# A sixth weight buffer in a three-layer float32 kernel, in SBUF given up by GpSimd's DMA scratch

## What is computed

```python
# twice (l = 0, 1)
mod = silu(c) @ w_ada[l] + b_ada[l]             # [2048] @ [2048, 6144]: shift, scale, gate
u = rms_norm(x, norm_w) * (1 + scale) + shift
proj = u @ w_in[l]                              # [256, 2048] @ [2048, 19064]
...                                             # two attentions, a state space scan, gates
merged = g0 * (y_fox @ w_o_fox) + g1 * (y_dsa @ w_o_dsa) + g2 * (y_ssd @ w_o_ssd)
x = x + gate * (merged @ w_out)
# once
z = rms_norm(x) @ w_in_2                        # [256, 2048] @ [2048, 13312]
...                                             # a two-sided recurrence, a windowed attention
x = x + rms_norm((m0 * (y_a @ w_proj_a) + m1 * (y_b @ w_proj_b)) @ w_out_2)
```

## Time and profile before

| | us |
|---|---|
| median of 3 runs | 3477.04 (3476.33 to 3477.14) |
| the profiled execution's own time | 3473.09 |
| its span on the profile | 3471.3 |
| PE busy | 3335.0 (96%) |
| DVE busy | 2238.9 (64%) |
| ACT busy | 1701.7 (49%) |
| POOL busy | 46.8 (1%) |
| load queue of SP | 675.38 MB, 52.5% of 16 DMA engines |

### The profile page before, as it was taken

The page is one execution under the profiler, slowest core; times in us unless marked ns, Lnnn a source line. Parts: engine busy times, 40 slices in busy tenths (PEclk is TensorE's granted clock), DMA queues, the critical chain, the costliest instruction groups (busy, mean ns, idle before and its releaser), DMA issues.

```text
span 3471.3 us, 43913 instructions
## 1 busy us (share of the span) xinstructions
PE 3335.0 (96%) x18250; PEld 2894.8 (83%) x18250; DVE 2238.9 (64%) x2687; ACT 1701.7 (49%) x2098; POOL 46.8 (1%) x90
## 2 busy tenths in 40 slices
PE   5799989989999999999999999999999999999998
PEld 4679978878888887799788878888888899988887
DVE  5688777866666556687666576655567776544544
ACT  3354565554434344546655544343446875434343
POOL 0000000000000000000000000000000000000000
PEclk8799999999999999999999999999999999999999
DMA  8654456556677655444544467765555443455554
GB/s 354 261 222 173 170 209 248 219 199 249 260 279 287 224 183 193 162 179 158 180 172 159 174 234 267 272 249 196 189 183 191 177 173 140 158 218 194 194 184 156
DMA packets 102918, 719.32 MB, mean 207 GB/s; under 512 B 12176, under 2 KB 12256, under 8 KB 18752
## 3 DMA queue, kind: packets, MB, share of 16 engines
q1 hardware_dynamic: 93888, 675.38, 52.5%
q0 software_dynamic: 8256, 37.64, 3.1%
q10 hardware_dynamic: 576, 3.50, 0.3%
HBM read 710.08 MB, written 6.40 MB: 206 GB/s over the span
## 4 chain that ended last, share of the span: by engine, by line
PE 86%; DVE 7%; ACT 3%; DMA 2%; issue 1%; SPq 0%; DVEq 0%; ACTq 0%
PE G L1214 79%; DVE LL L1812 3%; DMA RAW<-w_ada_turned_packed_dram 1%; PE BA L1362 1%; PE BD L1335 1%; DVE S L2019 1%; PE BD L1397 1%; DMA RAW<-in_w_in_packed_dram 1%; ACT HH L1455 1%; PE BC L1348 0%; DVE RAW L1823 0%; PE BE L1280 0%; PE BA L1416 0%; PE BC L1416 0%; PE BC L1380 0%
## 5 line engine op out<-in xcount | busy, mean ns | idle before, releaser
L1455 ACT ACTIVATE HH<-RAW 128x2048 fp32r<-128x2048 f32 x546 | 1044.7, 1914 | 1138.1 <-PE G L1214 838.4
L1812 DVE TENSOR_TENSOR LL<-RAW,HH 128x2048 fp32r<-128x2048 f32 x546 | 1247.8, 2287 | 357.8 <-ACT HH L1455 357.3
L1214 PE MATMUL G<-HH,UH 128*128 128x512 f32 x2560 | 1022.1, 399 | 61.2 <-DVE LL L1812 57.2
L1214 PE MATMUL G<-LL,UH 128*128 128x512 f32 x2560 | 1003.6, 392 | 0.0
L1214 PE MATMUL G<-HH,UL 128*128 128x512 f32 x2560 | 1003.3, 392 | 0.0
L1214 PEld LDWEIGHTS G<-HH,UH 128*128 128x128 f32 x2560 | 485.1, 189 | 171.0 <-DVE LL L1812 67.4
L1214 PE MATMUL G<-UH,HH 128*128 128x256 f32 x2080 | 602.9, 290 | 9.8 <-DVE XS L2055 7.2
L1214 PE MATMUL G<-UH,LL 128*128 128x256 f32 x2080 | 589.2, 283 | 0.0
L1214 PE MATMUL G<-UL,HH 128*128 128x256 f32 x2080 | 588.9, 283 | 0.0
L1214 PEld LDWEIGHTS G<-LL,UH 128*128 128x128 f32 x2560 | 484.5, 189 | 103.7
L1214 PEld LDWEIGHTS G<-HH,UL 128*128 128x128 f32 x2560 | 485.6, 190 | 100.6 <-issue 2.9
(11 more groups left out here) (336 smaller groups left out, 2304.2 us busy)
## 6 DMA issues: line engine op xcount, KB each, us to landing
RAW<-in_w_in_packed_dram SPq DMA_DIRECT2D x402, 1024.0 KB, 4.8
RAW<-w_ada_turned_packed_dram SPq DMA_DIRECT2D x88, 1024.0 KB, 4.9
RAW<-in_w_out_packed_dram SPq DMA_DIRECT2D x48, 1024.0 KB, 4.8
RAW<-in_w_o_ssd_packed_dram SPq DMA_DIRECT2D x32, 1024.0 KB, 4.8
RAW<-in_w_o_fox_packed_dram SPq DMA_DIRECT2D x16, 1024.0 KB, 4.8
RAW<-in_w_o_dsa_packed_dram SPq DMA_DIRECT2D x16, 1024.0 KB, 4.9
RAW<-in_w_proj_a_packed_dram SPq DMA_DIRECT2D x16, 1024.0 KB, 4.8
RAW<-in_w_proj_b_packed_dram SPq DMA_DIRECT2D x16, 1024.0 KB, 4.8
```

What stands on the lines that cost most here:

```text
L1214: mm = pe.matmul(to, lt, rh, start=first, stop=end, skip_group_check=True)
L1455: a.activation(HH[g % NH][:, :n], RAW[buf(ch["f"])][:, :n], ACT.Copy).then_inc(*hi_done.up(g))
L1812: v.tensor_tensor(LL[buf(f)][:, :n], RAW[buf(f)][:, :n], HH[g % NH][:, :n].bitcast(F32), ALU.subtract).then_inc(*lo_done.up(g))
```

## The change

```diff
@@ -28,7 +28,7 @@
 
 C_ID, C_PI, C_UM, C_CM, C_IF, C_ONE, C_FR, C_END = 0, 128, 256, 384, 640, 641, 642, 690
 
-NR, NX, NH = 5, 3, 3
+NR, NX, NH = 6, 3, 3
 
 
 ON_PE = 2
@@ -2466,7 +2466,7 @@
     import concourse.bacc as bacc
     from concourse.bass_utils import run_bass_kernel_spmd
 
-    nc = bacc.Bacc("TRN2", target_bir_lowering=False, num_devices=1)
+    nc = bacc.Bacc("TRN2", target_bir_lowering=False, num_devices=1, dynamic_dma_scratch_size=8192)
     arrays, args = {}, {}
     given = laid_out(inputs)
     for name, arr in given.items():
```

## The result

The changed kernel takes **3448.44 us** (median of 4 runs, 3447.71 to 3450.18), the kernel before beside it 3476.68 (4 runs, 3471.77 to 3477.14). The ratio is 0.9924, 95% interval 0.9912 to 0.9935. The profiled execution took 3450.18 us.

The account below looks back on a forecast made before the run. PE, busy 3335.0 of 3471.3 us, was taken as the bound, with only gaps ending in late loads winnable. 7.5 + 13.2 - 1.0 = 19.7 us off the median of 3477.0 gave 3457.3 us; range 3451 to 3470.

Parts of the forecast that it names:

- What bounds the kernel: Whole kernel: PE bounds it; a buffer wins only PE idle time ending with a late load, in the opening and layer 0.
- The opening: Groups two to four of the opening: each ends 2.52 us earlier as its last loads land sooner, 7.5 us in all.
- Layer 0: Six places in layer 0 where a chunk's late load reaches PE: 13.2 us in all.
- 2.0 of the 2.97 go: Chunk 54 in layer 0: 2.0 us of PE's gap of 2.97 us would go.
- I take 3.0: Chunk 89 in layer 0: PE's gap of 2.88 us goes whole, with a trace of the next, 3.0 us.
- Chunks 84, 93 and 107: Layer 0: gains of 0.6, 3.5 and 2.8 us on PE; the prediction called the middle one chunk 94.
- Chunk 15: Layer 0: of PE's gap of 2.55 us, 1.3 us would be won.
- Take off 1 for what I have missed: Layer 0's sum: 1 us subtracted from the gain for anything missed.
- 1: Rival: only the opening wins, as `HH` holds ACT back and DVE fills layer 0's gaps; 3469.5 us, chance 0.12.
- 2: Rival: only layer 0 wins, as PE's second dot or full DMA engines limit the opening; 3463.8 us, chance 0.10.
- 3: Rival: nothing to see, under 7 us in all, both gains at half strength; about 3473 us, chance 0.09.
- 4: Rival: slower, as POOL waits for room in the halved scratch during the state space scan; 3495 us, chance 0.05.

Follow-up runs that it names:

- x5: Changed kernel, but six layer 0 loads (for chunks 15, 54, 84, 89, 94 and 107) wait as with five buffers; 3466.29 us, 0.9974 of the kernel before.
- x7: Kernel before with its five weight buffers, and the 8 KB spent on a fourth `HH`; 3473.03 us, 0.9994 of the kernel before.
- x1: The changed kernel again, nothing altered, timed beside the kernel before; 3448.72 us, ratio 0.9926.
- x3: Changed kernel with the sixth buffer used in the opening alone, five buffers afterwards; 3465.76 us, 0.9975 of the kernel before.
- x6: Changed kernel, but load 96 alone (chunk 54) waits as it would with five buffers; 3458.86 us, 0.9953 of the kernel before.
- x9: x6 plus 24 matmuls for nobody, run by PE in the gap ahead of the late head's transposes; 3455.58 us, 0.9939 of the kernel before.
- x10: Changed kernel, but load 168 alone, the ada load ahead of chunk 107's, waits as with five buffers; 3452.98 us, 0.9933 of the kernel before.
- x2: Kernel before with five buffers, only the scratch cut to 8192 bytes; 3474.15 us, 0.9999 of the kernel before.
- x4: Changed kernel with the sixth buffer used only after the opening; 3456.55 us, 0.9948 of the kernel before.
- x11: x8 with five buffers in place of six; 3458.09 us, 0.9949 of the kernel before.
- x8: Changed kernel, but in the opening PE's first dot of the next group stands ahead of the group's gemm; 3437.96 us, 0.9894 of the kernel before.

## Why the prediction was too careful

**What bounds the kernel: right.** The split into places where a load reaches PE and places where `HH` holds ACT anyway is borne out by x5 (few loads carry all of layer 0) and x7 (the larger wait was worth nothing). Layers 1 and 2 didn't move, and the stretch from 860 to 1130 is as busy as it was.

**The opening: right.** 7.5 forecast, 7.1 measured, 7.7 in x1 and 7.8 in x3. The fourth gemm starts at 126.48 in place of 134.19 (7.71 earlier) and ends only 6.81 earlier: it now runs more of its time at the low clock (0.60 on average in the 8 us from its start, against 0.74 before, in the windows above).

**Layer 0: the step that failed.** The text had "PE wins what lies behind it up to its next limit" and took the length of a gap as its price. That mis-sized two terms, "2.0 of the 2.97 go" at chunk 54 and "I take 3.0" at chunk 89. Measured are 5.1 and 4.8. By idle time alone both would be 2.5, close to the text; the rest is the halved clock behind each gap, 0.57 to 0.84 in the windows of before and 1.00 after. x6 brought gap and clock back at chunk 54 (5.4 us), x9 the gap without the clock (3.2). Chunks 84, 93 and 107 came as forecast (0.9, 3.3, 3.1 against 0.6, 3.5, 2.8). At 84 and 107 there was no low clock. At 93 idle time went from 6.4 us to 3.3, and a stretch at half clock of 3.4 us remains in place of 6.8; next to nothing came of that, as 3.1 of the 3.3 are idle time. Two of these hits are partly luck, as the two places also vary among kernels whose loads wait as before: 107 by 1.3 to 1.7 us (x10), 93 by 1.4 (x2, x3). Chunk 15 was put at 1.3 and gave -0.5 or 1.1, by where the stretch at low clock fell. Chunks 51 and 63 gave back 0.3 and 0.5, since a stretch at low clock came to them. The clock stood among the rows, and no term of the sum priced it.

**"Take off 1 for what I have missed": wrong in sign.** What was missed lay on the other side. Layer 0 was 12.2 with it and 15.8 by the trace, the whole 19.7 against 22.9.

**The scale: 4 us.** The text added the distance of one profiled execution of before to a median of three runs (3473.1 to 3477.0) to the result. After the change the profiled execution lies 1.7 us above its median, so 5.7 of the 8.9 us between 3457.3 and 3448.44 are this offset, and 3.2 are the sum's. In 19, 21 and 9 further runs the kernel before had medians of 3474.98, 3475.53 and 3475.76, from 3471.4 to 3480. The offset was scatter, not a property to carry over, and the low end of the range should have allowed for it.

**The rivals.** 1 and 2 fell by x3 and x4, 3 by the result, 4 by x2. The Trainium skill's rule on the descriptor carveout ("Debugging Trainium Hangs", section 4) didn't come into play: with 8192 bytes for 64 transfers the kernel ran in the same time (x2). No run shows how full the area was.

## What to carry to other kernels

Look for what a wait holds up, not at its size: 544 of 838 us of waits went for nothing (x7), and a few of the 299 us of waits for loads were worth 16. Where a late step makes TensorE idle in otherwise dense work (some 3 us here), price the gap at its length plus the stretch at low clock behind it, and see in the windows whether the granted clock is low there now. Before a buffer is spent on a load that waits for an instruction, see whether that instruction can be moved into an idle stretch: in the opening that alone was worth 17.6 us (x11), the buffer alone 7.8 (x3).

## What the hardware showed that I had not expected

- A gap of about 3 us on TensorE was followed by a granted clock of 0.50 for 6.8 us (from 476.1 before, from 469.9 in x6). Matmuls that keep it busy for nobody take that away (x9). The Trainium skill ("TensorE: Matmul & The Clock Gate", Terms) puts the penalty at the throttled time times one half. By that page an estimate for 6.8 us is 3.4. Measured were 2.2 (x9 against x6) to 2.6 (chunk 54). PE was idle for 1.1 us of that time in any case, which takes 0.6 off, and in x9 its next wait grew from 1.08 us to 1.53; with both the estimate is 2.4.
- What a stretch at low clock costs depends on what lies in it. Ahead of a wait it cost nothing, behind it 1.6 us more, in two profiles of one kernel (x1).
- The clock also falls in some executions and not in others. In x10 and x11 it did at gemm 290, in layer 1, behind a PE gap of 2.02 us that the changed kernel, x1, x4 and x8 have too, at full speed. First x10, then the changed kernel:

```profile
1928.00:1934.00 6.00, 6.00 (x40) 6.00 (x39) 3.58 (x3) 1.54 (x2) 0.00 (x0) 0.72 0.24 101
```

```profile
1928.00:1934.00 6.00, 4.94 (x41) 4.97 (x42) 3.96 (x5) 2.48 (x3) 0.00 (x0) 1.00 0.39 161
```

  Each such stretch cost about 1.5 us at its gemm, of which a later wait sometimes gave the whole back. x11 has four that x8 has not, and lost 4.9 us behind gemm 198, where nothing distinguishes the two but the buffer. They are likely a part of why one kernel's runs spread over 3471 to 3480 us: the mean granted clock of the 3480.0 run of before was 0.979, of the shortest ones 0.982. What decides them was not tried.
